# First quarters of the adaLN modulation as TensorE strip matmuls instead of VectorE multiply-adds, first stage re-ordered

## What is computed

```python
c_act = jax.nn.silu(c)                                  # (1, 1024)
mod = c_act @ ada_w[l] + ada_b[l]                       # (1, 6*1024)
sh_m, sc_m, g_m, sh_f, sc_f, g_f = jnp.split(mod, 6, axis=-1)
h = rms_norm(x, norm_mix_g[l]) * (1 + sc_m) + sh_m      # the modulated input
u = h @ w_in                                            # (512, 3*1024), split into b_g, c_g, xv
...                                                     # conv, gate, MLP, attention layer, MLP
```

## Time and profile before

| | |
|---|---|
| median of 3 runs | 1216.71 us (1215.61 to 1218.96) |
| the profiled execution | 1218.56 us |
| its span in the trace | 1215.8 us |
| start of the first block product | 23.19 us |
| start of the first product after the stage (block of L792) | 61.60 us |

### The profile page before, as it was taken

The page is one execution under the profiler, slowest core; times in us unless marked ns, Lnnn a source line. Parts: engine busy times, 40 slices in busy tenths (PEclk is TensorE's granted clock), DMA queues, the critical chain, the costliest instruction groups (busy, mean ns, idle before and its releaser), DMA issues.

```text
span 1215.8 us, 17089 instructions
## 1 busy us (share of the span) xinstructions
PE 1186.3 (98%) x5891; PEld 996.9 (82%) x5891; DVE 765.6 (63%) x1117; ACT 500.9 (41%) x818; POOL 24.8 (2%) x37
## 2 busy tenths in 40 slices
PE   6999999999999999999999999999999999999998
PEld 5788888988878778888968888888888888888886
DVE  5557788875565565565879888886853443443441
ACT  5422332542232232333577788763632332331421
POOL 2000000000000000002020000000000000000000
PEclk8899999999999999999999999999999999999999
DMA  9587564466665666423245554450332333323332
GB/s 317 157 255 232 178 196 139 151 179 177 203 192 164 196 201 185 118 86 88 71 122 135 125 140 107 122 140 19 104 104 87 104 92 98 103 87 104 89 102 87
DMA packets 231697, 168.75 MB, mean 139 GB/s; under 512 B 5620, under 2 KB 214684, under 8 KB 231644
## 3 DMA queue, kind: packets, MB, share of 16 engines
q1 hardware_dynamic: 231452, 167.92, 47.9%
q0 software_dynamic: 32, 0.07, 0.0%
q10 hardware_dynamic: 160, 0.06, 0.0%
HBM read 153.24 MB, written 2.10 MB: 128 GB/s over the span
## 4 chain that ended last, share of the span: by engine, by line
PE 71%; DVE 10%; DMA 7%; ACT 4%; issue 4%; SPq 1%; DVEq 1%; ACTq 0%
PE bank L590 21%; PE bank L592 21%; PE bank L591 21%; DMA raw<-in_mlp_w 7%; DVE ada_acc L1719 2%; ACT w_hi L1078 2%; PE bank L937 2%; PE bank L919 1%; PE bank L909 1%; DVE w_lo L1496 1%; PE bank L910 1%; DVE ta L1536 1%; DVE x L1764 1%; DVE tc L1536 1%; SPq L398 1%
## 5 line engine op out<-in xcount | busy, mean ns | idle before, releaser
L590 PE MATMUL bank<-h_hi,w_hi 128*128 128x512 f32 (+1 forms) x888 | 338.1, 381 | 4.9 <-DVE w_lo L1496 1.9
L1078 ACT ACTIVATE w_hi<-raw 128x1024 fp32r<-128x1024 f32 x187 | 196.7, 1055 | 336.2 <-DMA raw<-in_mlp_w 289.7
L591 PE MATMUL bank<-h_lo,w_hi 128*128 128x512 f32 (+1 forms) x888 | 333.6, 376 | 0.0
L592 PE MATMUL bank<-h_hi,w_lo 128*128 128x512 f32 (+1 forms) x888 | 333.6, 376 | 0.0
L1496 DVE TENSOR_TENSOR w_lo<-raw,w_hi 128x1024 fp32r<-128x1024 f32 x187 | 228.1, 1223 | 139.7 <-ACT w_hi L1078 137.0
L590 PE MATMUL bank<-g_hi,w_hi 128*128 128x512 f32 (+1 forms) x688 | 261.0, 379 | 2.9 <-DVE g_lo L1820 2.9
L592 PE MATMUL bank<-g_hi,w_lo 128*128 128x512 f32 (+1 forms) x688 | 257.9, 375 | 0.0
L591 PE MATMUL bank<-g_lo,w_hi 128*128 128x512 f32 (+1 forms) x688 | 257.6, 374 | 0.0
L590 PEld LDWEIGHTS bank<-h_hi,w_hi 128*128 128x128 f32 x888 | 167.8, 189 | 40.3 <-issue 6.9
L592 PEld LDWEIGHTS bank<-h_hi,w_lo 128*128 128x128 f32 x888 | 168.0, 189 | 30.2
L591 PEld LDWEIGHTS bank<-h_lo,w_hi 128*128 128x128 f32 x888 | 168.1, 189 | 28.9 <-issue 0.5
(11 more groups left out here) (208 smaller groups left out, 1038.5 us busy)
## 6 DMA issues: line engine op xcount, KB each, us to landing
raw<-in_mlp_w SPq DMA_DIRECT2D x128, 512.0 KB, 4.2
ada_raw<-in_ada_w SPq DMA_DIRECT2D x40, 1024.0 KB, 5.4
raw<-in_sc_w_in SPq DMA_DIRECT2D x23, 512.0 KB, 6.0
ada_first<-in_ada_w SPq DMA_DIRECT2D x32, 256.0 KB, 7.2
raw<-in_w_kv SPq DMA_DIRECT2D x16, 512.0 KB, 4.0
raw<-in_sc_w_out SPq DMA_DIRECT2D x8, 512.0 KB, 4.0
raw<-in_q_w SPq DMA_DIRECT2D x8, 512.0 KB, 4.9
keys<-qk SPq DMA_DIRECT2D x16, 256.0 KB, 3.1
```

What stands on the lines that cost most here:

```text
L590: mm(out[:, cols], weights_hi, hi[:, k, cols], start=(k == 0), stop=False)
L591: mm(out[:, cols], weights_hi, lo[:, k, cols], start=False, stop=False)
L592: return mm(out[:, cols], weights_lo, hi[:, k, cols], start=False, stop=(k == KT - 1))
L1078: go(w_hi[:, jj, :, :], raw[:, jj, :, :], ACT.Copy).then_inc(hi_ok, 1)
```

## The change

VectorE's multiply-adds go. For each k of each quarter TensorE does one fp32 matmul with 32 weight columns and 512 moving columns: the weights are `c_wide[:, k, :]` (column 0 is `c_act[:, k]`, the other 31 are zero), the moving operand is the row group of `ada_first`. It writes 32 partitions of bank 6: k and k+4 share the strip of 32 array columns number k mod 4, so four strips hold partial sums. VectorE copies the whole bank to `ada_rows` (128 x 512), and `quarter_sum` sums over its partitions with the same four matmuls with a column of ones as before. The transfers of quarters 2 and 3 now wait for TensorE's matmul on the buffer (`ada_rows_pe`) instead of the VectorE step. The weights of blocks 0 to 2 are loaded between quarters 0 and 1, block 3 after quarter 1. The orders of the three engines are re-written around this.

```diff
 def ada_quarter(q):
     for k in range(KT):
-        if (q - 2, k) in STEP_NO:
-            sp.wait_ge(ada_stepped, STEP_NO[q - 2, k] + 1)
-        elif q >= 2:
-            sp.wait_ge(ada_direct, DIRECT_NO[q - 2, k] + 1)
+        if q >= 2:
+            sp.wait_ge(ada_rows_pe, (q - 2) * KT + k + 1)
...
 for q in range(QUARTERS):
     ada_quarter(q)
-    if q < 2:
-        load_block(2 * q, c_g(2 * q))
-        load_block(2 * q + 1, c_g(2 * q + 1))
+    for b in ((0, 1, 2), (3,), (), ())[q]:
+        load_block(b, c_g(b))
...
-def quarter_direct(q):
-    if q:
+def quarter_rows(q, first, last):
+    if q and first == 0:
         pe.wait_ge(ada_red, q)
-    for k in ADA_DIRECT[q]:
+    for k in range(first, last):
         pe.wait_ge(ada_in[q % 2][k], 16 * (q // 2 + 1))
-        for n in range(4):
-            one = mm(bank[6][:, n:n + 1], ada_first[:, q % 2, k, n // 2, n % 2 * P:(n % 2 + 1) * P],
-                     c_act[:, k:k + 1], start=(k == ADA_DIRECT[q][0] and n == 0), stop=False, ...)
-        one.then_inc(ada_direct, 1)
+        strip = slice(32 * (k % 4), 32 * (k % 4) + 32)
+        mm(bank[6][strip, :], c_wide[:, k, :], ada_first[:, q % 2, k, :, :], start=(k < 4), stop=(k >= 4),
+           skip_group_check=True).then_inc(ada_rows_pe, 1)
 def quarter_sum(q):
-    pe.wait_ge(ada_stepped, STEP_NO[q, ADA_STEPS[q][-1]] + 1)
+    pe.wait_ge(ada_rows_ok, q + 1)
     for n in range(4):
-        one = mm(bank[6][:, n:n + 1], ada_acc[:, c * P:(c + 1) * P], ones[:, 0:1], start=False, ...)
+        one = mm(bank[6][:, n:n + 1], ada_rows[:, n * P:(n + 1) * P], ones[:, 0:1], start=(n == 0), ...)
```

TensorE's order, before and after:

```diff
-x_turn(0) x_turn(1) x_turn(2) x_turn(3) x_turn(4)
-quarter_direct(0)  unit_pair(0)  quarter_sum(0)  x_turn(5)
-open_block(0, Q[0])  unit_pair(1)  quarter_direct(1)  quarter_sum(1)  open_block(1, Q[0])  x_turn(6)
-open_block(0, Q[1])  open_block(1, Q[1])  unit_pair(2)  quarter_direct(2)  quarter_sum(2)
-open_block(2, Q[0])  open_block(2, Q[1])  open_block(3, Q[0])  x_turn(7)  open_block(3, Q[1])
-open_block(0, Q[2])  open_block(1, Q[2])  unit_pair(3)  quarter_direct(3)  quarter_sum(3)
-open_block(2, Q[2])  open_block(3, Q[2])  blocks 0 and 1 on Q[3]  blocks 2 and 3 on Q[3]
+x_turn(0) rows(0, k=0)  x_turn(1) rows(0, k=1)  x_turn(2) rows(0, k=2)  x_turn(3) rows(0, k=3)
+rows(0, k=4,5)  unit_pair(0)  rows(0, k=6,7)  x_turn(4)  quarter_sum(0)
+open_block(0, Q[0])  unit_pair(1)  open_block(1, Q[0])  open_block(2, Q[0])
+rows(1)  x_turn(5)  quarter_sum(1)  open_block(0, Q[1])
+rows(2)  unit_pair(2)  open_block(1, Q[1])  quarter_sum(2)  open_block(2, Q[1])
+rows(3)  open_block(3, Q[0])  unit_pair(3)  quarter_sum(3)  open_block(3, Q[1])
+open_block(0, Q[2])  open_block(1, Q[2])  open_block(2, Q[2])  open_block(3, Q[2])
+x_turn(6)  blocks 0 and 1 on Q[3]  x_turn(7)  blocks 2 and 3 on Q[3]
```

VectorE:

```diff
+nc.vector.memset(c_wide[:], 0.0).then_inc(wide_zero, 1)
...
 tt(c_act[:], cols[:, R_C:R_C + KT], c_tmp[:], ALU.mult).then_inc(c_ok, 1)
+dve.wait_ge(wide_zero, 1)
 dve.wait_ge(c_ok, 1)
-quarter_steps(0, 0, 2)
+nc.vector.tensor_copy(c_wide[:, :, 0:1], c_act[:].rearrange("p (k a) -> p k a", a=1)).then_inc(c_ok, 1)
...
+def quarter_copy(q):
+    dve.wait_ge(ada_rows_pe, (q + 1) * KT)
+    nc.vector.tensor_copy(ada_rows[:], bank[6][:]).then_inc(ada_rows_ok, 1)
...
-quarter_steps(0, 2, 5)  split(0, 0)  quarter_gain(0)  quarter_steps(1, ...) and so on
+quarter_copy(0)  quarter_gain(0)  split(0, 0)  first_low(0)  first_low(1)  split(0, 1)  split(0, 2)
+quarter_copy(1)  quarter_gain(1)  first_low(2)  first_low(3)  split(0, 3)
+quarter_copy(2)  quarter_gain(2)  first_low(4)  first_low(5)
+quarter_copy(3)  quarter_gain(3)  first_low(6)  first_low(7)  split_early()
```

More of the change, by code:

```diff
@@ L52 @@
 X_BANK = [0, 1, 2, 3, 7, 7, 7, 7]
[L55 to L58, removed]
 KVQ_ORDER = [("k", 0), ("v", 0), ("k", 1), ("q", 0), ("q", 1), ("v", 1)]
@@ L165, in yoco_trunk @@
     raw, = stacked(region_w, [("raw", [P, GROUP, KT, P], F32)])
-    rms = new("rms", [P, T], F32)
+    region_rms = region(size([P, T], F32))
+    rms, = stacked(region_rms, [("rms", [P, T], F32)])
+    ada_rows, = stacked(region_rms, [("ada_rows", [P, T], F32)])
     ssum = new("ssum", [P, T], F32)
@@ L178, in yoco_trunk @@
     sq_hi, = stacked(region_tc + size([P, T], F32), [("sq_hi", [P, T], F32R)])
-    tv = new("tv", [P, T], F32)
+    region_tv = region(size([P, T], F32))
+    tv, = stacked(region_tv, [("tv", [P, T], F32)])
+    c_wide, = stacked(region_tv, [("c_wide", [P, KT, 32], F32)])
     ident = new("ident", [P, P], F32)
@@ L242, in yoco_trunk @@
         c_ok = sem("c_ok")
-        ada_stepped = sem("ada_stepped")
-        ada_direct = sem("ada_direct")
+        wide_zero = sem("wide_zero")
+        ada_rows_pe = sem("ada_rows_pe")
+        ada_rows_ok = sem("ada_rows_ok")
         ada_used = sem("ada_used")
@@ L710, in unit_pair @@
                     v.then_inc(unit_turned, 1)
-            def quarter_direct(q):
-                if q:
+            def quarter_rows(q, first, last):
+                if q and first == 0:
                     pe.wait_ge(ada_red, q)
-                for k in ADA_DIRECT[q]:
+                for k in range(first, last):
                     pe.wait_ge(ada_in[q % 2][k], 16 * (q // 2 + 1))
-                    for n in range(4):
-                        one = mm(bank[6][:, n:n + 1], ada_first[:, q % 2, k, n // 2, n % 2 * P:(n % 2 + 1) * P],
-                                 c_act[:, k:k + 1], start=(k == ADA_DIRECT[q][0] and n == 0), stop=False,
-                                 skip_group_check=True)
-                    one.then_inc(ada_direct, 1)
+                    strip = slice(32 * (k % 4), 32 * (k % 4) + 32)
+                    mm(bank[6][strip, :], c_wide[:, k, :], ada_first[:, q % 2, k, :, :], start=(k < 4), stop=(k >= 4),
+                       skip_group_check=True).then_inc(ada_rows_pe, 1)
             def quarter_sum(q):
-                pe.wait_ge(ada_stepped, STEP_NO[q, ADA_STEPS[q][-1]] + 1)
+                pe.wait_ge(ada_rows_ok, q + 1)
                 for n in range(4):
-                    c = n // 2 * KT + 2 * q + n % 2
-                    one = mm(bank[6][:, n:n + 1], ada_acc[:, c * P:(c + 1) * P], ones[:, 0:1], start=False,
+                    one = mm(bank[6][:, n:n + 1], ada_rows[:, n * P:(n + 1) * P], ones[:, 0:1], start=(n == 0),
                              stop=True, skip_group_check=True)
@@ L751, in _ @@
             pe.wait_ge(cols_ok, 2)
-            pe.wait_ge(c_ok, 1)
+            pe.wait_ge(c_ok, 2)
             Q = [range(2 * q, 2 * q + 2) for q in range(QUARTERS)]
-            for j in range(5):
+            for j in range(4):
                 x_turn(j)
-            quarter_direct(0)
+                quarter_rows(0, j, j + 1)
+            quarter_rows(0, 4, 6)
             unit_pair(0)
+            quarter_rows(0, 6, KT)
+            x_turn(4)
             quarter_sum(0)
-            x_turn(5)
             pe.wait_ge(x_ok, 4)
@@ L762, in _ @@
             unit_pair(1)
-            quarter_direct(1)
+            open_block(1, Q[0])
+            open_block(2, Q[0])
+            quarter_rows(1, 0, KT)
+            x_turn(5)
             quarter_sum(1)
-            open_block(1, Q[0])
-            x_turn(6)
             open_block(0, Q[1])
+            quarter_rows(2, 0, KT)
+            unit_pair(2)
             open_block(1, Q[1])
-            unit_pair(2)
-            quarter_direct(2)
             quarter_sum(2)
-            open_block(2, Q[0])
             open_block(2, Q[1])
+            quarter_rows(3, 0, KT)
             open_block(3, Q[0])
-            x_turn(7)
+            unit_pair(3)
+            quarter_sum(3)
             open_block(3, Q[1])
@@ L778, in _ @@
             open_block(1, Q[2])
-            unit_pair(3)
-            quarter_direct(3)
-            quarter_sum(3)
             open_block(2, Q[2])
             open_block(3, Q[2])
+            x_turn(6)
             for tile in Q[3]:
@@ L786, in _ @@
                     open_block(b, range(tile, tile + 1))
+            x_turn(7)
             open_block(2, Q[3])
@@ L1188, in split_early @@
                 go(early_hi[:], early_raw[:], ACT.Copy).then_inc(hi_ok, 1)
+            for j in range(4):
+                x_tile(j)
             split(0, 0)
-            for j in range(5):
-                x_tile(j)
             first_tile(0)
@@ L1195, in _ @@
             split(0, 1)
+            x_tile(4)
+            split(0, 2)
             x_tile(5)
@@ L1198, in _ @@
             first_tile(3)
-            split(0, 2)
-            x_tile(6)
             split(0, 3)
@@ L1203, in _ @@
             first_tile(5)
-            x_tile(7)
-            split_early()
             first_tile(6)
             first_tile(7)
+            x_tile(6)
+            split_early()
+            x_tile(7)
             act.wait_ge(unit_rest_ok, TT - 2)
```

21 lines of the change are left out of this document (6 added, 15 removed).

## The result

Ten runs of each kernel on the same chips: before 1217.36 us, after 1222.90 us, ratio 1.0037 with a 95% interval of 1.0026 to 1.0049. The change makes the kernel slower by 4.5 us (3.2 to 6.0). The direction was right and the time lies in the range of 1219 to 1246, but the change had been forecast as 16.1 us, over three times what came.

A forecast was written before the change was run, and what follows sets the result against it. TensorE's list in the first stage bounds the kernel. First product at 26.9 us, then 28.5 work, 11.6 strips, 4.7 waits, 6.0 clock: 50.8; stage ends at 77.7, 16.1 later, so 1232.8 us, range 1219 to 1246.

The forecast's parts named there:

- What bounds the kernel: First stage: TensorE's list sets the pace, VectorE's work lies beside it; the 1154 us behind the stage stay unchanged.
- The price of the strips: Strip matmuls: only neighbouring k overlap, n matmuls take n+1 passes; eight 3.9 us, three quarters 11.6 us.
- four at the price of one: Rival on the strip matmuls: passes of different strips all overlap; +8.8 us, 1225.5 us, chance 0.20.
- Until the first product: Start to first block product: start 10.2 us, clock rises at 17.1, first product at 26.9, 3.7 us later.
- The waits behind the sums: Behind the first product: TensorE waits for quarter 1's 3.06 us chain, the copy and second tiles; together 4.7 us.
- The clock term: Behind the first product: two stretches without dense work keep the clock loss at 6.0 us, as before.
- Queues: Transfers: quarter 3 issued after TensorE's rows of quarter 1, some 33 us, needed past 50; delays covered.

The follow-up runs named there:

- the one-strip run: Changed kernel with all eight k of a quarter on the same 32 array columns, sum over 32 partitions: 1241.69 us, ratio 1.0192.
- the two-strip run: Changed kernel with two strips instead of four (k modulo 2), sum over 64 partitions: 1229.12 us, ratio 1.0107.
- the grouped kernels: Changed kernel, wait behind quarter_sum(1) filled, quarter 0's strip matmuls grouped, block 2 loaded after quarter 1: 1215.64 us; with block 2's low part behind quarter 1's copy: 1215.88.

## Why the prediction was wrong

- **What bounds the kernel: right.** Only the end of the first stage moved; the 14 us less of VectorE brought nothing, and what is behind the stage stayed at 1154.
- **The price of the strips: the step that failed.** I put "the second pass of k with the first of k+1", nine passes for eight matmuls, 3.9 us, argued from rows that all use the whole array and start in program order. Measured 1.85: four strips at the price of one. What failed is the order of the passes: four passes start together, then four more, and no second pass stands alone between them. Over three quarters 5.6 instead of 11.6, 6.0 us of the error. The rival "four at the price of one" was right on this price; the one-strip run and the two-strip run show that it is the number of strips. I had given it 0.20 and its time as 1225.5, which is still too slow, as it keeps the forecast waits and most of the slow start.
- **Until the first product: too slow.** I had 26.9, the trace 24.52. TensorE started at 9.76, not 10.2, the clock rose not at 17.1 but by the second strip matmul (1.84 us at 10.78, 0.97 at 13.65), and k = 4 to 7 took no third pass. 2.4 us. As this start differs between executions by up to 1.5 us, part of it may be chance. The forecast time of the rise rested on a loose reading too: the stretch "30.75 to 37.5" is counted from where the clock fell, not from where products began (30.05 us in the trace before).
- **The waits behind the sums: right in kind.** The chain behind `quarter_sum(1)` showed as 2.87 us, with 0.3 for the copy; all idle behind the first product 3.2, forecast 4.7. 1.5 us.
- **The clock term: right as a remainder, too big as a price.** 43.6 less 3.2 idle less 34.1 of work (28.5 + 5.6) is 6.3 us, forecast 6.0. But where the clock was 1.00 throughout, with the wait filled and unused matmuls ahead of the first product, TensorE was busy for 35.9 us with this same work (36.77 from 25.91 to 62.68, less 0.85 idle). So some 1.8 us of the remainder are work that my prices leave out, and 4.5 the clock.
- **What the loss is made of.** By the same prices, and therefore as an estimate, the stage behind the first product grew by 5.2 us. Of these 3.6 are more TensorE work (5.6 of strips for 2.4 of direct matmuls, and one `x_turn` that used to lie ahead), 1.3 more idle time, and 0.3 clock; the other 1.3 of the 6.5 lie ahead of the first product. The clock loss and most of the idle time are thus not new: the kernel before had them too. Filling the wait does not undo the cause; the strips' work is still paid there and is made up by less idle time and a better clock.
- **Queues: right.** The transfers of quarter 3 were issued until 37.6 us, the loads stood nearly still at 33 to 34 us (9 GB/s), and no wait for it followed. What I did not see is that VectorE's copy would be the fragile place in its queue; that showed only when the loads were moved.

The sum: 16.1 less 6.0, 2.4 and 1.5 is 6.2; with the 0.3 more of the clock term that is the 6.5 of the trace.

## What to carry to other kernels

Price packed matmuls on different column strips as one, also for fp32 with its two passes, and then compare with what they replace on the engine that limits: here 5.6 us of TensorE for 2.4 of TensorE and some 18 us of an engine off the path. Look at what stands behind them in TensorE's queue: here filling a wait of 2.9 us shortened the stage by 6.0, more than double, as the clock had fallen in it. Put independent products there before anything else. When a producer moves to another engine, the copy it needs becomes a new item in a queue: place it ahead of anything that waits for a load.

## What was not expected of the hardware

- An fp32 matmul of 512 columns on a strip of 32 array columns takes its two passes like any other, 0.87 us in a series, and four on four strips take them together: eight in 7.0, 3.6 and 1.85 us on one, two and four strips.
- What TensorE did before the clock changed. In the changed kernel it was at 1.2 GHz in the first strip matmul (1.84 us at 10.78) and at 2.4 in the second (0.97 at 13.65), with transposes ahead of and between them. In the kernel before, 20 transposes alone, 4.2 us of them, all ran at 1.2 GHz. With strip matmuls in both long waits the granted clock was 1.00 through the stage. With early strip matmuls in the kernel before, the clock was high for 20 transposes; then TensorE idled 1.67 us and ran 24 one-column matmuls from 13.92, and during these the clock fell (granted clock 0.97 from 13.9 to 16.0, 0.50 from 16.0 to 17.0). No run separates that wait from the kind of matmul behind it.
- The same list of instructions got its full clock at different times in different executions: the twelve transposes of the grouped kernels took 1.5 to 2.6 us.
- The clock column reads 1.00 at the start, where the pace of the transposes (0.21 us each, 0.12 with TensorE kept busy before) shows 1.2 GHz.
